# A weighted one-hot row made on GpSimd, and the plain one by one wide compare on VectorE

## The reference

```
s = einsum('thpd,hpkd->thpk', q, sub_keys)         # 8 heads, 2 halves, 128 keys
s_top, i_top = top_k(s, 16)                        # per half
cand = s_top[:, :, 0, :, None] + s_top[:, :, 1, None, :]
best, pos = top_k(cand, 16)                        # per head, of 256 pairs
eid = i_top0 * 128 + i_top1  at pos                # the expert's number
gate = softmax(best)
act = gelu(einsum('td,thkd->thk', xt, u_tab[eid]))
out = einsum('thk,thkd->td', gate * act, v_tab[eid])
```

## Time and profile before

| | |
|---|---|
| median of 3 runs | 3798.87 us (3798.09 to 3800.53) |
| the profiled execution | 3799.12 us, span 3797.4 us |
| TensorE busy | 3336.8 us, 88% |
| VectorE busy | 2432.4 us, 64% |
| ScalarE busy | 1498.4 us, 39% |
| GpSimd busy | 426.0 us, 11% |
| DMA | 511.74 MB, 134 GB/s from HBM over the span |

### The profile page before, as it was taken

How to read it: one execution, slowest core, us unless ns; L and a number is a source line. 1 busy time by engine, 2 the same in 40 slices (tenths; PEclk the granted TensorE clock), 3 DMA queues, 4 the chain that set the end, 5 groups by cost and what they waited for, 6 DMA issues and landing times. The chain is left out here.

```text
span 3797.4 us, 59274 instructions
## 1 busy us (share of the span) xinstructions
PE 3336.8 (88%) x20672; PEld 2901.2 (76%) x20672; DVE 2432.4 (64%) x4939; ACT 1498.4 (39%) x2306; POOL 426.0 (11%) x460
## 2 busy tenths in 40 slices
PE   6888999999977687999999967966679799999995
PEld 5777899999874576899999963864358689999994
DVE  4689666666655589666666655553148966666663
ACT  4237444444342227444444432221223744444443
POOL 0257000000000058000000000000005800000000
PEclk8999999999988899999999988988789999999997
DMA  4411555555441320555555531001143045555552
GB/s 195 160 57 30 184 186 187 188 188 188 172 154 59 128 100 1 177 185 185 185 186 187 188 142 63 1 1 33 45 158 103 1 165 185 185 186 187 187 188 92
DMA packets 126706, 511.74 MB, mean 135 GB/s; under 512 B 14704, under 2 KB 15344, under 8 KB 119152
## 3 DMA queue, kind: packets, MB, share of 16 engines
q1 hardware_dynamic: 126576, 510.07, 37.4%
HBM read 508.96 MB, written 1.05 MB: 134 GB/s over the span
## 5 line engine op out<-in xcount | busy, mean ns | idle before, releaser
L406 PE MATMUL ps<-xh,uhigh 128*128 128x256 f32 x3072 | 871.0, 284 | 14.6 <-POOL ulow L788 14.6
L408 PE MATMUL ps<-xh,ulow 128*128 128x256 f32 x3072 | 869.8, 283 | 0.0
L407 PE MATMUL ps<-xl,uhigh 128*128 128x256 f32 x3072 | 869.7, 283 | 0.0
L406 PEld LDWEIGHTS ps<-xh,uhigh 128*128 128x128 f32 x3072 | 588.3, 192 | 32.5 <-POOL ulow L788 19.6
L407 PEld LDWEIGHTS ps<-xl,uhigh 128*128 128x128 f32 x3072 | 588.4, 192 | 12.9
L408 PEld LDWEIGHTS ps<-xh,ulow 128*128 128x128 f32 x3072 | 588.4, 192 | 0.0
L753 DVE TENSOR_TENSOR ulow<-stream,uhigh 128x1024 fp32r<-128x1024 f32 x330 | 404.4, 1225 | 201.4 <-ACT uhigh L531 201.4
L531 ACT CAST uhigh<-stream 128x1024 fp32r<-128x1024 f32 x336 | 352.7, 1050 | 433.8 <-DMA stream<-in_u 433.8
L424 PE MATMUL ps<-vhigh,chigh 128*128 128x512 f32 x1536 | 480.3, 394 | 4.7 <-DVE vlow L769 4.3
L758 DVE TENSOR_TENSOR stream<-stream,big 128x256 f32<-128x256 f32 x336 | 218.0, 649 | 404.1 <-ACT stream L589 403.9
L424 PE MATMUL ps<-vlow,chigh 128*128 128x512 f32 x1536 | 476.2, 391 | 0.0
(11 more groups left out here) (417 smaller groups left out, 4353.9 us busy)
## 6 DMA issues: line engine op xcount, KB each, us to landing
stream<-in_u SPq DMA_DIRECT2D x384, 512.0 KB, 4.2
stream<-in_v SPq DMA_DIRECT2D x369, 512.0 KB, 3.5
big<-in_wq SPq DMA_DIRECT2D x24, 1152.0 KB, 7.8
stream<-in_ab_w_in SPq DMA_DIRECT2D x4, 2048.0 KB, 11.4
stream<-in_c_w_qf SPq DMA_DIRECT2D x16, 512.0 KB, 3.6
stream<-in_c_w_ig SPq DMA_DIRECT2D x4, 2048.0 KB, 8.2
big<-in_w_gates SPq DMA_DIRECT2D x4, 2048.0 KB, 8.0
spare<-in_v SPq DMA_DIRECT2D x15, 512.0 KB, 3.4
```

The source lines that it names most:

```text
L406: pe.matmul(out, uh[:, b, cols], c.xh[:, k, :], start=k == 0, stop=False)
L407: pe.matmul(out, uh[:, b, cols], c.xl[:, k, :], start=False, stop=False)
L408: ins = pe.matmul(out, ul[:, b, cols], c.xh[:, k, :], start=False, stop=k == KD - 1)
```

## The change

In quads whose B is made by GpSimd the weight moves from A to B: GpSimd compares and multiplies in each of its four instructions, and VectorE makes A by one wide compare without the weight. In quads that VectorE makes whole, A is the wide compare and B is made by four narrow ones with the weight. In ScalarE's quads nothing changes. The string of makers becomes PAPAPD, repeated and cut to 64, so GpSimd has 32 quads (as before), ScalarE 22 (before 24) and VectorE 10 (before 8). GpSimd waits for the weights too.

```diff
-    MAKER = "DPAPAPAP"
-    made = lambda g: sum(MAKER[x % 8] == MAKER[g % 8] for x in range(g + 1))
+    MAKER = ("PAPAPD" * QUADS)[:QUADS]
+    made = lambda g: MAKER[:g + 1].count(MAKER[g])
...
+            for g in range(2):
+                if MAKER[g] == "A":
+                    act_keys(g)
             for g in range(QUADS):
-                if MAKER[(g + 2) % 8] == "A" and g + 2 < QUADS:
+                if g + 2 < QUADS and MAKER[g + 2] == "A":
                     act_keys(g + 2)
...
-                if MAKER[g % 8] == "D":
-                    dve.tensor_tensor(B[:, g % 4], bc(c.iota, 1, 4), bc(c.selt[:, 1, 4 * g:4 * g + 4], 2, P), ALU.is_equal)
-                for q in range(4):
-                    t = 4 * g + q
-                    ins = dve.tensor_scalar(A[:, g % 4, q, :], c.iota[:], c.selt[:, 0, t:t + 1], c.selt[:, 2, t:t + 1],
-                                            ALU.is_equal, ALU.mult)
+                if MAKER[g] == "A":
+                    for q in range(4):
+                        t = 4 * g + q
+                        ins = dve.tensor_scalar(A[:, g % 4, q, :], c.iota[:], c.selt[:, 0, t:t + 1],
+                                                c.selt[:, 2, t:t + 1], ALU.is_equal, ALU.mult)
+                else:
+                    ins = dve.tensor_tensor(A[:, g % 4], bc(c.iota, 1, 4), bc(c.selt[:, 0, 4 * g:4 * g + 4], 2, P),
+                                            ALU.is_equal)
+                if MAKER[g] == "D":
+                    for q in range(4):
+                        t = 4 * g + q
+                        ins = dve.tensor_scalar(B[:, g % 4, q, :], c.iota[:], c.selt[:, 1, t:t + 1],
+                                                c.selt[:, 2, t:t + 1], ALU.is_equal, ALU.mult)
                 ins.then_inc(a_ready, 1)
...
-            alone(selt_ready, 1)
+            alone(selt_ready, 2)
...
-                    ins = pool.tensor_scalar(B[:, g % 4, q, :], c.iota[:], c.selt[:, 1, t:t + 1], None, ALU.is_equal)
+                    ins = pool.tensor_scalar(B[:, g % 4, q, :], c.iota[:], c.selt[:, 1, t:t + 1], c.selt[:, 2, t:t + 1],
+                                             ALU.is_equal, ALU.mult)
```

More of the change, by code:

```diff
@@ L457, in _ @@
                 pe.wait_ge(a_ready, g + 1)
-                if MAKER[g % 8] == "A":
+                if MAKER[g] == "A":
                     pe.wait_ge(act_b_ready, made(g))
-                elif MAKER[g % 8] == "P":
+                elif MAKER[g] == "P":
                     pe.wait_ge(b_ready, made(g))
@@ L806, in _ @@
                 early_low(n)
-            alone(selt_ready, 1)
+            alone(selt_ready, 2)
             for g in range(QUADS):
-                if MAKER[g % 8] != "P":
+                if MAKER[g] != "P":
                     continue
```

## The result

The changed kernel takes 3854.90 us (median of 4, 3852.69 to 3859.32) against 3799.25 before on the same chip: ratio 1.0148, 95% interval 1.0130 to 1.0165, so 55.7 us slower. I had forecast 3787.3 with a range of 3774 to 3838; the time lies above the range, on the side of the first rival, and beyond the price I gave that one (3822).

What follows compares the result with a forecast made beforehand. VectorE was taken to bound the peer-stage loops, with GpSimd next; GpSimd's 2.34 + 0.39 + 0 = 2.73 us a quad saves 3.9 us a loop, 11.7 in three, giving 3787.3 us, range 3774 to 3838.

Steps and rivals of the forecast that it cites:

- the first rival: GpSimd's narrow instruction: the second operation costs time, 0.09 us each giving 3822 (pointer read alone 3820); chance 0.32.
- VectorE bounds the loop, GpSimd is next: Quad loops of the peer stages: VectorE falls from 90.6 to 73.8 us, then GpSimd bounds with 87.4.
- the sum: GpSimd's time per quad, running without gaps: 2.34 + 0.39 + 0 = 2.73 us, 87.4 us a loop.
- Term 3: GpSimd's second operation with its pointer: taken as 0 us, between -0.02 and 0.30 an instruction.
- Term 2: Delays of GpSimd by VectorE: 1.31 wide compares a quad at 0.22 us, plus 0.1, making 0.39 us.
- best case: Three peer-stage loops with the second operation at no cost: 3.9 us gained a loop, 11.7 in all.
- ScalarE and TensorE under the bound: In each loop ScalarE falls from 80.5 to 76.6 us and TensorE keeps 75.3, both below GpSimd.
- The second rival: Wide compares hold GpSimd up more, mean wait 0.40 us: 94.9 us a loop, 3810; chance 0.13.
- The third: GpSimd is hardly delayed: 2.34 us a quad, TensorE bounds, 3766, or 3769 half-way; chance 0.12.
- my own case: GpSimd bounds the loops at 2.73 us a quad: 3787.3, range 3781 to 3795, chance 0.43.

Runs made afterwards that it cites:

- PAD: The changed kernel with the string of makers PAD (22 GpSimd, 21 ScalarE, 21 VectorE quads a loop), against the kernel before: ratio 1.0012 (1.0003 to 1.0021).

## Why the prediction was wrong

- *VectorE bounds the loop, GpSimd is next.* Right. VectorE's busy time fell by 13.3 us, and my sum in steps was 16.8. GpSimd had no gap in the loops, as the sum took it.
- *Term 3, the second operation at 0.* This step failed. It is 0.198 us an instruction (0.577 to 0.775): 384 x 0.198 = 76 us, where I had put nothing. My sign for the first rival was a step of 0.61 or more. The two experiments that add and remove it alone, +51 us and back to 0.9995, show it as the cause. Between the traces without and with it the loops grow by 66 us and not 76, because the delays by VectorE shrink by 6 and GpSimd's gaps by 2. The fault was in how I placed it between the ends of -0.02 and 0.30. From the 0.58 against L794's 0.30 I concluded that much of the instruction was fixed and might already hold the new parts. The fixed part is 0.25, and a new pointer adds to it (0.086) instead of hiding in it; the columns cost 2.5 ns each, and a second operation adds 0.9. Both parts that I named, pointer and multiply, cost; I had given them a single price of 0.09 even in the rival.
- *Term 2, delays by VectorE.* Right in size: the mean step is 0.872, which is 0.097 over the undisturbed one, 0.39 us a quad, the value of the sum. The steps that a wide compare touches hold 31.0 us of these delays for 126 compares, 0.25 each (0.22 in the sum); the other steps hold 6.3, 0.07 a quad (0.1 in the sum). With one operation the delay was 0.11, 0.45 a quad, so the mean does not carry over from one kernel to another, and that the two parts, one above and one below the sum, meet at 0.39 is luck.
- *The sum with the one term put right.* 2.34 + 0.39 + 4 x 0.198 = 3.52 us a quad, 112.7 us; GpSimd's loop measured 111.9, 111.1 and 111.9. By the sum the kernel would be 64 us slower; the loops show 59. Of the other 5, 3 are the sum's 112.7, 1 the tail (TensorE's last two quads in 2.02 us instead of 2.5, three times) and 1 GpSimd's later start, which the loops as measured leave out.
- *The size of the best case.* Too large as well. With the operation free, 11.7 us were forecast and 2.0 (-1.5 to 5.7) measured. The GpSimd quad was 2.79 for 2.73, 2 us a loop of the 3.9. The loops of the traces show 7.9 us of gain (281.8 to 273.9), and the medians less. What lies outside the loops takes between 3510 and 3526 us in the traces of this case, 3516 in that of the kernel before and 3522 in this one; that covers the difference without explaining it.
- *ScalarE and TensorE under the bound.* Right, 72.4 and 68.3 us of 114. TensorE's busy time is under my 75.3 for the same matmuls; quads now often run in twos, 2.02 us for both, where one alone has 1.16.
- *Rivals.* The first was the right mechanism at under half its size. Its estimate by the Trainium skill (GPSIMD Engine Reference, "Performance pitfalls for Q7 kernels"), 3820, priced the pointer at 0.085 us, which measured 0.083 to 0.086, and left the operation out. The second rival, wide compares, is real but was in the sum already. The third did not occur.
- *Chances.* The range ended at a price of 0.13 although the bounds ran to 0.30: with the upper end at 3900 in hand and no row between, it should have reached further. In the range of my own case the 3781 was wrong by its own sum: a mean wait of 0.14 us gives 3777, and 3781 belongs to 0.17.

## What to carry to other kernels

Work that is moved from the bounding engine to one with 9% of slack must be priced on the engine that gets it; if no row shows the new form there, the forecast's centre is a guess, and a run of that form by itself comes first. On an engine with a fixed cost and a cost by column, look for both in anything that is added. And sums of busy time by engine are a floor: with VectorE and GpSimd busy 84 us each and four places between them, PAD's loop came out at 94.1, 8 us above its sum. Where an engine waits for two producers, compare its start with the end of each; the name in the view can be that of the wrong one.

## What the hardware showed

- GpSimd's `tensor_scalar` of 128 partitions, fp32: 0.25 us and 2.5 ns a column with one operation and a pointer; a second operation 0.9 ns a column; a second pointer 0.083 to 0.086 us.
- A GpSimd instruction that starts within a VectorE compare of two SBUF inputs (128 x 512) goes on about 0.56 us after the compare began: +0.20, +0.35 and +0.49 us for starts 0.35, 0.21 and 0.08 into it. One that began 0.08 before the compare was held up as well (+0.55); one that began 0.23 before was not.
- ScalarE's activation of 128 x 128 takes 0.39 us from start to start with pointers for scale and bias (1.56 for four), where the wide one of 128 x 512 is 0.72 long.
